# Five PE transpositions of a macaron decoder layer handed to VectorE: spatial weights, memory, and three residual halves

## The reference, cut to what matters

```python
h = h + 0.5 * _swiglu(_rmsnorm(h, g_ffn1[l]), w_ffn1_in[l], w_ffn1_out[l])
z = _rmsnorm(h, g_mix[l]) @ w_mix_in[l]
gate_b, gate_c, h_c, u, v = jnp.split(z, splits, axis=-1)
y_conv = gate_b * _causal_dwconv(gate_c * h_c, conv_w[l], conv_b[l])
y_gm = _spatial_gating(u, v, g_gm_v[l], w_spatial[l], b_spatial[l])
h = h + jnp.concatenate([y_conv, y_gm], axis=-1) @ w_mix_out[l]
h = h + _cross_attention(_rmsnorm(h, g_xattn[l]), _rmsnorm(mem, g_mem[l]), w_xq[l], w_xk[l], w_xv[l], w_xo[l])
h = h + 0.5 * _swiglu(_rmsnorm(h, g_ffn2[l]), w_ffn2_in[l], w_ffn2_out[l])
return _rmsnorm(h, g_final)
```

## Time and profile before

| what | value |
|---|---|
| median of three runs | 2165.45 us |
| the profiled execution's own time | 2165.3 us |
| its span, first to last instruction | 2163.5 us |
| granted TensorE clock, mean | 0.998 |
| PE busy | 2143.0 us, 99% |
| PEld busy | 1778.5 us, 82% |
| DVE busy | 1349.1 us, 62% |
| ACT busy | 991.4 us, 46% |
| DMA, mean | 191 GB/s |

### The profile page before, as it was taken

One profiled execution on the slowest core, in us unless ns is written; L12 is line 12 of the kernel. 1 busy time (PEld: TensorE's weight loads), 2 busy tenths in 40 slices (PEclk: granted clock), 3 DMA queues, 4 the chain that ended last, 5 costly groups with the idle time before them and its releaser, 6 DMA issues.

```text
span 2163.5 us, 25558 instructions
## 1 busy us (share of the span) xinstructions
PE 2143.0 (99%) x9626; PEld 1778.5 (82%) x9626; DVE 1349.1 (62%) x1549; ACT 991.4 (46%) x1103; POOL 1.8 (0%) x7
## 2 busy tenths in 40 slices
PE   8999999999999999999999999999999999999998
PEld 6888888888888888888888888888888888888886
DVE  5677667766475547865677554576677667764544
ACT  5444444444344544444554444454444444443433
POOL 0000000000000000000000000000000000000000
PEclk9999999999999999999999999999999999999999
DMA  6666666665556566665556545466666666665664
GB/s 226 213 187 200 194 191 190 193 197 193 193 181 207 182 196 185 197 220 181 181 169 212 165 158 175 161 217 195 194 187 196 193 193 192 194 196 193 194 194 138
DMA packets 159217, 412.20 MB, mean 191 GB/s; under 512 B 12588, under 2 KB 13732, under 8 KB 158756
## 3 DMA queue, kind: packets, MB, share of 16 engines
q1 hardware_dynamic: 157728, 410.04, 60.8%
q10 hardware_dynamic: 1412, 1.11, 0.2%
HBM read 409.01 MB, written 2.10 MB: 190 GB/s over the span
## 4 chain that ended last, share of the span: by engine, by line
PE 96%; DVE 2%; ACT 1%; DMA 0%; issue 0%; ACTq 0%; DVEq 0%
PE ps L911 94%; PE ps L940 1%; DVE w_lo L580 1%; PE ps L924 1%; DVE ps L640 1%; DVE convT L753 0%; DMA h<-in_x 0%; DVE xT_lo L588 0%; ACT xT_hi L334 0%; ACT w_hi L326 0%; ACT convT L449 0%; PE ps L1028 0%; DVE stage L743 0%; ACT scratch L560 0%; ACT zT L446 0%
## 5 line engine op out<-in xcount | busy, mean ns | idle before, releaser
L580 DVE TENSOR_TENSOR w_lo<-raw,w_hi 128x1024 fp32r<-128x1024 f32 x768 | 935.9, 1224 | 750.5 <-ACT w_hi L326 745.1
L326 ACT ACTIVATE w_hi<-raw 128x1024 fp32r<-128x1024 f32 x768 | 811.5, 1061 | 1080.7 <-PE ps L911 1051.0
L911 PE MATMUL ps<-w_hi,xT_hi 128*128 128x512 f32 x1856 | 573.8, 390 | 5.3 <-DVE w_lo L580 5.3
L911 PE MATMUL ps<-w_hi,xT_lo 128*128 128x512 f32 x1856 | 571.9, 389 | 0.0
L911 PE MATMUL ps<-w_lo,xT_hi 128*128 128x512 f32 x1856 | 571.9, 389 | 0.0
L911 PEld LDWEIGHTS ps<-w_hi,xT_hi 128*128 128x128 f32 x1856 | 347.8, 188 | 79.0 <-issue 4.0
L911 PEld LDWEIGHTS ps<-w_lo,xT_hi 128*128 128x128 f32 x1856 | 348.8, 188 | 72.6
L911 PEld LDWEIGHTS ps<-w_hi,xT_lo 128*128 128x128 f32 x1856 | 348.6, 188 | 72.6
L911 PE MATMUL ps<-w_hi,hidT_hi 128*128 128x512 f32 x704 | 218.2, 389 | 0.4 <-DVE w_lo L580 0.4
L911 PE MATMUL ps<-w_lo,hidT_hi 128*128 128x512 f32 x704 | 218.1, 389 | 0.0
L911 PE MATMUL ps<-w_hi,hidT_lo 128*128 128x512 f32 x704 | 218.0, 389 | 0.0
(11 more groups left out here) (119 smaller groups left out, 801.2 us busy)
## 6 DMA issues: line engine op xcount, KB each, us to landing
raw<-in_w_ffn_in SPq DMA_DIRECT2D x352, 512.0 KB, 4.1
raw<-in_w_ffn_out SPq DMA_DIRECT2D x176, 512.0 KB, 4.5
raw<-in_w_mix_in SPq DMA_DIRECT2D x80, 512.0 KB, 3.8
raw<-in_w_mix_out SPq DMA_DIRECT2D x32, 512.0 KB, 3.8
raw<-in_w_xq SPq DMA_DIRECT2D x32, 512.0 KB, 4.4
raw<-in_w_xk SPq DMA_DIRECT2D x32, 512.0 KB, 4.3
raw<-in_w_xv SPq DMA_DIRECT2D x32, 512.0 KB, 3.8
raw<-in_w_xo SPq DMA_DIRECT2D x32, 512.0 KB, 3.8
```

The source lines that it names most:

```text
L326: nc.scalar.activation(w_hi[:, k % RING, :], raw[:, k % RAW, :], ACT.Copy).then_inc(hi_ready, 1)
L580: nc.vector.tensor_tensor(w_lo[:, k % RING, :], raw[:, k % RAW, :], w_hi[:, k % RING, :].bitcast(F32), ALU.subtract).then_inc(lo_ready, 1)
L911: ins = nc.tensor.matmul(bank(s, t * GW + b * BLK, BLK), xs[:, k, t * P:(t + 1) * P], ws_[:, k % RING, b * BLK:(b + 1) * BLK], start=(k == ...
```

## The change

Five pieces of turning leave TensorE.

- `ws` is turned in group `H` by 16 VectorE instructions straight from SBUF to SBUF, four ahead of each of the units 4 to 7. The two copies go.
- `mix_out0` is turned by VectorE during `mix_out1`, with the existing `by_dve=True`.
- The memory is turned by VectorE from SBUF to SBUF into a new tensor `memT_nat` (`turn_mem`): 16 instructions of 32x512 for each half, two ahead of each of the units 8 to 15, the first half in `mix_out0`, the second in `q0`. Its rounding by ScalarE (`hi_mem`) comes in `mix_out1` around unit 13 and at the start of `q1`; its low part by VectorE (`lo_mem`) in `mix_out1` between units 13 and 14, and in `q1` behind unit 12.
- `ffn1_out1` and `xo1` are turned by VectorE in two parts (`resid_turned`), 32 instructions of 32x256: 16 of them at once between `add_resid` and unit 4, the others in fours ahead of units 8, 9, 10 and 11.

```diff
+            def resid_turned(name, c, dst, g, first, half):
+                hi_units(first, 0, 4)
+                act.wait_ge(staged, STAGED[name] + TOK)
+                squares(h, c, name)
+                hi_units(first, 4, 7)
+                hi_scaled(dst, c * HALF, g, half, name, 0, 2)
+                hi_units(first, 7, 12)
+                hi_scaled(dst, c * HALF, g, half, name, 2, 4)
...
             u = UNIT0["mix_out1"]
-            resid("mix_out0", 0, xT_hi, "g_xattn", u, SET["mix_out0"])
-            hi_units(u, 8, 13)
-            hi_scaled(memT_hi, 0, "g_mem", SET["mix_out0"], "memA")
-            hi_units(u, 13, KD)
+            resid("mix_out0", 0, xT_hi, "g_xattn", u, SET["mix_out0"], LATE)
+            hi_mem(0, 0, 4)
+            hi_units(u, LATE, LATE + 1)
+            hi_mem(0, 4, HALF)
+            hi_units(u, LATE + 1, KD)
...
             u = UNIT0["q1"]
-            hi_units(u, 0, 4)
+            hi_mem(1, 0, 4)
+            hi_units(u, 0, 2)
+            hi_mem(1, 4, HALF)
+            hi_units(u, 2, 4)
...
+            def turn_mem(c, u, k0):
+                for i in range(8):
+                    turn_sbuf(memT_nat[:, c * HALF:(c + 1) * HALF, :], mem_nat[:, :, c * GW:(c + 1) * GW], mem_turned,
+                              2 * i, 2 * i + 2)
+                    lo_units(u, k0 + i, k0 + i + 1)
...
+            def resid_turned(name, c, coef, g, u):
+                lo_units(u, 0, 4)
+                add_resid(name, c, coef)
+                src = h[:, :, c * GW:(c + 1) * GW]
+                dve.wait_ge(staged, STAGED[name] + TOK)
+                turn_blocks(src[:, :, 0:BLK], SET[name], HALF // 2, 0, 16)
+                lo_units(u, 4, 6)
+                lo_scaled(xT_lo, xT_hi, c * HALF, g, SET[name], name, 0, 2)
+                lo_units(u, 6, 8)
+                for i in range(4):
+                    turn_blocks(src[:, :, BLK:GW], SET[name], HALF // 2, 4 * i, 4 * i + 4, HALF // 2)
+                    if i < 3:
+                        lo_units(u, 8 + i, 9 + i)
+                lo_units(u, 11, 12)
+                lo_scaled(xT_lo, xT_hi, c * HALF, g, SET[name], name, 2, 4)
+                lo_units(u, 12, 14)
...
             u = UNIT0["mix_out1"]
-            resid("mix_out0", 0, 1.0, "g_xattn", u)
-            lo_units(u, 8, 13)
-            lo_scaled(memT_lo, memT_hi, 0, "g_mem", SET["mix_out0"], "memA")
-            lo_units(u, 13, KD)
+            resid("mix_out0", 0, 1.0, "g_xattn", u, by_dve=True)
+            lo_units(u, LATE, LATE + 1)
+            lo_mem(0)
+            lo_units(u, LATE + 1, KD)
...
-            lo_units(u, 8, 13)
-            lo_scaled(memT_lo, memT_hi, HALF, "g_mem", SET["mix_out1"], "memB")
-            lo_units(u, 13, KD)
+            turn_mem(1, u, 8)
...
                 if c == 0:
+                    lo_mem(1)
                     dve.wait_ge(squared, SQUARED["mem1"] + 2)
                     norm("mem", halves, D, rstd_mem[:, :])
...
-            resid("ffn1_out1", 1, "C", xT_hi, xT_lo, TAKEN["ffn1_out0"] + 4)
+            pe.wait_ge(taken, TAKEN["ffn1_out0"] + 4)
+            group("C", xT_hi, xT_lo, 0, 8)
+            pe.wait_ge(taken, TAKEN["ffn1_out1"] + 2)
+            group("C", xT_hi, xT_lo, 8, 12)
             pe.wait_ge(taken, TAKEN["ffn1_out1"] + 4)
-            group("C", xT_hi, xT_lo, 8, 9)
-            pe.wait_ge(ws_masked, 1)
-            for hd in range(HEADS):
-                ins = nc.tensor.transpose(bank(SET["ffn1_out1"], hd * P, P), ws[:, hd, :], ident[:, :])
-                if hd % 4 == 3:
-                    ins.then_inc(turned, 1)
-            group("C", xT_hi, xT_lo, 9, KD)
+            group("C", xT_hi, xT_lo, 12, KD)
...
             pe.wait_ge(taken, TAKEN["q0"] + 4)
+            pe.wait_ge(mem_split, KD)
```

More of the change, by code:

```diff
@@ L335, in hi_scaled, with hi_mem @@
                     ins.then_inc(hi_taken, 1)
+            def hi_mem(c, k0, k1):
+                act.wait_ge(mem_turned, c + 1)
+                for k in range(c * HALF + k0, c * HALF + k1):
+                    nc.scalar.activation(memT_hi[:, k, :], memT_nat[:, k, :], ACT.Copy,
+                                         scale=col("g_mem", k)).then_inc(mem_hi, 1)
             def hi_plain(dst, k0, s, banks, ready, first, b0=0):
@@ L643, in turn_blocks, with turn_sbuf, lo_mem @@
                         ins.then_inc(turned, tiles // 2)
+            def turn_sbuf(dst, src, landed, n0, n1):
+                dst = dst.rearrange("p k (t b) -> p t k b", t=TOK)
+                src = src.rearrange("p t (k c) -> p t k c", c=P)
+                for n in range(n0, n1):
+                    q, j = n // 4, n % 4
+                    ins = nc.vector.transpose(dst[j * Q:(j + 1) * Q, :, :, q * Q:(q + 1) * Q],
+                                              src[q * Q:(q + 1) * Q, :, :, j * Q:(j + 1) * Q])
+                    if n == 15:
+                        ins.then_inc(landed, 1)
+            def turn_mem(c, u, k0):
[3 more added lines that the diff above has]
+                    lo_units(u, k0 + i, k0 + i + 1)
+            def lo_mem(c):
+                for k in range(c * HALF, (c + 1) * HALF):
+                    dve.wait_ge(mem_hi, k + 1)
+                    nc.vector.scalar_tensor_tensor(out=memT_lo[:, k, :], in0=memT_nat[:, k, :], scalar=col("g_mem", k),
+                                                   in1=memT_hi[:, k, :].bitcast(F32), op0=ALU.mult,
+                                                   op1=ALU.subtract).then_inc(mem_split, 1)
+            def resid_turned(name, c, coef, g, u):
[14 more added lines that the diff above has]
+                lo_units(u, 12, 14)
             def turn_between(name, src, u):
@@ L726, in _ @@
             u = UNIT0["C"]
-            resid("ffn1_out1", 1, 0.5, "g_mix", u)
+            resid_turned("ffn1_out1", 1, 0.5, "g_mix", u)
             dve.wait_ge(squared, SQUARED["ffn1_out1"] + 2)
             norm("ffn1", halves, D, rstd[:, :])
-            lo_units(u, 8, 13)
[L731 to L734, removed]
-            lo_units(u, 13, KD)
-            lo_units(UNIT0["H"], 0, KD)
+            lo_units(u, 14, KD)
+            u = UNIT0["H"]
+            lo_units(u, 0, 4)
+            dve.wait_ge(ws_masked, 1)
+            for n in range(16):
+                q, j = n // 4, n % 4
+                ins = nc.vector.transpose(wsT[j * Q:(j + 1) * Q, :, q * Q:(q + 1) * Q],
+                                          ws[q * Q:(q + 1) * Q, :, j * Q:(j + 1) * Q])
+                if n % 4 == 3:
+                    lo_units(u, 4 + q, 5 + q)
+            ins.then_inc(ws_turned, 1)
+            lo_units(u, 8, KD)
             u = UNIT0["B"]
@@ L1041, in _ @@
             group("mix_out0", yT_hi, yT_lo, 8, KD)
-            resid("mix_out0", 0, "mix_out1", yT_hi, yT_lo, TAKEN["U"] + 4)
-            group("mix_out1", yT_hi, yT_lo, 8, 9)
-            pe.wait_ge(taken, TAKEN["mix_out0"] + 4)
-            pe.wait_ge(mem_loaded, 16)
-            turn(from_half(mem_nat, 0), SET["mix_out0"], HALF)
-            group("mix_out1", yT_hi, yT_lo, 9, KD)
-            resid("mix_out1", 1, "q0", xT_hi, xT_lo, TAKEN["memA"] + 4)
+            pe.wait_ge(taken, TAKEN["U"] + 4)
+            group("mix_out1", yT_hi, yT_lo, 0, KD)
+            resid("mix_out1", 1, "q0", xT_hi, xT_lo, TAKEN["mix_out0"] + 4)
             pe.wait_ge(taken, TAKEN["mix_out1"] + 4)
-            group("q0", xT_hi, xT_lo, 8, 9)
-            turn(from_half(mem_nat, 1), SET["mix_out1"], HALF)
-            group("q0", xT_hi, xT_lo, 9, KD)
+            group("q0", xT_hi, xT_lo, 8, KD)
             def turned_group(name, T_hi, T_lo, before, running, k1):
@@ L1119, in _ @@
             group("xo1", yT_hi, yT_lo, 0, KD)
-            resid("xo1", 1, "ffn2_in0", xT_hi, xT_lo, TAKEN["xo0"] + 4)
+            pe.wait_ge(taken, TAKEN["xo0"] + 4)
+            group("ffn2_in0", xT_hi, xT_lo, 0, 8)
+            pe.wait_ge(taken, TAKEN["xo1"] + 2)
+            group("ffn2_in0", xT_hi, xT_lo, 8, 12)
             pe.wait_ge(taken, TAKEN["xo1"] + 4)
-            group("ffn2_in0", xT_hi, xT_lo, 8, KD)
+            group("ffn2_in0", xT_hi, xT_lo, 12, KD)
             ffn_in(2)
```

45 lines of the change are left out of this document (24 added, 21 removed).

## The result

The changed kernel takes 2169.52 us (median of 17 runs, 2168.99 to 2170.79), the kernel before in the same sessions 2165.45 (17 runs, 2164.90 to 2166.78): 4.07 us or 0.18% more, ratio 1.0018 with a 95% interval of 1.0011 to 1.0025. The profiled execution has a span of 2168.2 us, 4.7 more than the one before.

What follows compares the result with a forecast made beforehand. TensorE, busy 99% of the span and almost without gaps, was taken as the bound. Its terms, -9.72 + 2 x 2.92 + 2.75 + 2.86 = +1.73 us, gave 2167.2 against the median of 2165.45; range 2162.5 to 2172.5.

Steps and rivals of the forecast that it cites:

- the bounds of the forecast alone: Whole kernel: 2165.7 to 2169.5 us, with waits 0.3 us shorter or longer at each place.
- What leaves TensorE, 9.72 us: TensorE: five pieces of sixteen transpositions at 1.76 us and eight of the spatial weights at 0.92 go, 9.72 us off.
- C and ffn2_in0, 2.92 us each: Before unit 4: sixteen turnings in one piece delay w_lo, a wait of 2.82 us plus 0.10 restart in each group.
- Unit 12 was in time, as held: C and ffn2_in0: unit 12 is ready 1.3 us early, so no wait.
- H, mix_out0 and q0 at nothing: Turnings of weights and memory ahead of units there cost TensorE zero; up to +2 us for the range.
- the bounds for a dearer one: q0: turnings may each be 0.17 us dearer before TensorE waits; each 0.1 beyond costs 1.6 us.
- mix_out1, 2.75 us: Before units 13 and 14: waits of 1.10 and 1.45 us, with restarts 1.20 and 1.55, together 2.75.
- q1, 2.86 us: Before unit 13: lo_mem delays all by 3.22 us, a wait of 2.76, with restart 2.86.
- The sum of the waits, +1.73: Whole kernel: -9.72 + 2 x 2.92 + 2.75 + 2.86 = +1.73 us.
- a rival, 13 in 100, 2172.2: Waits in C, q1 and ffn2_in0 each drop TensorE's clock, 3 x 1.7 = 5 us more: 2172.2; 13 in 100.
- The rival that all is hidden, 5 in 100: Whole kernel: VectorE has room for all the moved work, no new waits, 2155.6 us; 5 in 100.
- The rival of more waits on VectorE: Thin leads at unit 12 in C and ffn2_in0, and in q0, give further waits: 2170.2 us; 13 in 100.

Runs made afterwards that it cites:

- placed: Kernel before with weights, memory and mix_out0 turned by VectorE, the memory's roundings and low parts placed in idle time or behind unit 14 of q1; 2158.73 us.
- spread: placed with ffn1_out1 and xo1 also turned by VectorE, first part in pieces of 8, 4 and 4 ahead of units 4, 5 and 6; 2159.29 us.
- q1_split: placed with four of the memory's eight second low parts behind unit 12 of q1, the other four behind unit 14; 2160.13 us.
- halves_ws: Kernel before with spatial weights, ffn1_out1 and xo1 turned by VectorE, the last two in two parts; 2168.32 us, ratio 1.0012.
- lo_mem_late: Changed kernel with the memory's second low part made behind unit 14 of q1 instead of behind unit 12; 2166.87 us.
- q1_only: placed with the memory's whole second low part made behind unit 12 of q1 again, as in the change; 2162.49 us.
- q1_only_2: The kernel of q1_only, unedited, profiled once more; 2162.50 us.
- change_2: Changed kernel, unedited, profiled a second time; no median given, TensorE's stretch +3.5 us against the kernel before.
- change_3: Changed kernel, unedited, profiled a third time; no median given, TensorE's stretch +5.3 us against the kernel before.

## Why the prediction was right, and what it missed

The measured 2169.52 lies in the range of 2162.5 to 2172.5, and the change is within 0.2% as forecast, but 2.3 us above the forecast of 2167.2. It is at the very edge of the bounds of the forecast alone (2165.7 to 2169.5), and their upper end is more than the rule given with them explains: 0.3 us at each of five places makes 2168.7. So the number owes part of its success to a wide range; the mechanism of the waits owes it nothing.

- **What leaves TensorE, 9.72 us:** right. The 88 transpositions are gone, and placed, which keeps 6.2 us of it without a new wait, has 6.2 less in TensorE's stretch and measures 6.84.
- **C and ffn2_in0, 2.92 us each:** right. They are 2.81 with 0.1 behind it. Sixteen turnings take 7.50 us, by the working 7.52. Unit 12 was in time, as held.
- **H, mix_out0 and q0 at nothing:** right, no wait there. The turning from SBUF to SBUF, which no row had shown, takes 703 ns for 32x512 and 436 for 32x256, 20 less than into PSUM, so the bounds for a dearer one were never tried.
- **mix_out1, 2.75 us:** 1.30 (by the working 1.10) and 1.45 with 0.1 each, 2.95. Four roundings from SBUF take 1.75 us, not 1.51.
- **q1, 2.86 us:** 2.72 with 0.1 behind it. The eight low parts took 3.25.
- **The sum of the waits, +1.73:** 1.9, and 2.0 by TensorE's stretch. This part of the prediction held to 0.3 us.
- **The clock:** here the forecast failed. It took one of two cases, all three long waits followed by half rate (a rival, 13 in 100, 2172.2) or none (the forecast). The three profiled executions of the changed kernel show one, one and two drops. At 1.6 us each that is 2.1 us on the mean, and 1.9 + 2.1 = 4.0 is near the measured 4.07; it rests on three executions, and the unequal ends of the executions are not in it. The step that was wrong is to price the clock at zero in the likeliest case and to treat it as all or nothing. Its evidence was thin: a wait of 0.7 us without half rate, and the half rate at the start. The latter is no drop behind a wait: in every trace the first products run so, and only then does the clock rise for the first time. The price of a drop, 1.7 us by the earlier trace rows, was right all the same. That the gaps are short beside dense work, which the prediction took as speaking for no drop by the Trainium skill's rule that activity lifts the throttle (TensorE: Matmul & The Clock Gate, Part 1), did not help: the traces show drops behind waits of 2.7 us in the midst of dense work (86 us of it, without a new wait, before the wait of q1).
- **The rival that all is hidden, 5 in 100:** false for the order of the change. placed shows that for the memory, mix_out0 and the weights it can be had. For the two halves spread removes the long wait but keeps 1.4 us of short ones in each; whether a third order could do without them was not tried.
- **The rival of more waits on VectorE:** false, q0 and unit 12 kept their lead.

The rule to turn 128x128 by TensorE (the Trainium skill, VectorE: DVE Perf Modes, "Rules for kernel authors") stood against the change as a whole. The runs draw the line elsewhere: by engine time VectorE is six to seven times dearer (11.6 us against 1.76), but where its time is idle anyway, three of the five pieces and the weights are gained in full.

## What to carry to other kernels

When the bounding engine has no gap, lay a clock of due times over it and walk the feeding engine's queue instruction by instruction: each moved piece gains its full time or costs the lateness of the next thing behind it, and that was worked out to 0.2 us before a run here. Put moved work where the timeline already shows that engine waiting, not at the end of a stage where its lead is used up; the same pieces cost 4.1 us in one order (the change) and gained 6.9 in another (spread). Price a new gap of TensorE at its length and, from somewhere between 1.45 and 2.7 us in these runs, with a chance of 1.6 us for the clock on top. Two gaps of half the length are safer than one: eight waits of 1.3 to 1.45 us in mix_out1 and one of 1.1 in q1_split had no drop behind them, seven of fifteen of 2.7 to 2.8 had. And compare profiled executions between two fixed instructions, past the start and short of the end: differences of 1 us that the medians don't settle can be read there.

## What the hardware showed that I had not expected

- Half rate can come late: behind a wait of 2.7 us in q1 of the changed kernel, TensorE ran 1.5 us at the full rate before four pairs at 0.85 us instead of 0.45. It need not: in halves_ws it came 0.2 us behind the wait and in lo_mem_late with the first matmul. With a wait of 4.5 us it was there with the first pair and lasted for five more.
- The same wait in the same kernel is followed by half rate in one execution and not in the next (q1_only and q1_only_2; ffn2_in0 in change_2 and change_3).
- The first products of this kernel run at half rate for three to seven pairs, different in each execution, and the start alone moves an execution by up to 2.2 us. (The windows view gives 1.00 for this stretch, because the trace has no record of the clock before its rise, which is at 13.07 us in the kernel before; the pairs at 0.85 us show it.)
- VectorE's turning from SBUF to SBUF costs 20 ns less than into PSUM (703 and 723 ns for 32x512), and ScalarE's scaled copy of 128x256 costs more from SBUF (four in 1.75 us) than from PSUM (eight in 3.03 us).
